# Gate and up units of the feed-forwards' groups 4 to 11 with seven products of quarters, their weight sums on VectorE

## The chip, the cores and the metric

The kernel runs on one core of one Trainium2 chip, in one launch. The metric is the device time of that core in microseconds (us), the median of several executions.

## The reference

Two transformer blocks follow each other on 512 tokens of 1024 features, with 16 further "meta" tokens ahead of them. Each block is a mixer (retention and stick-breaking heads in the first, two causal convolutions in the second) and then a feed-forward part. Everything is float32. The change touches only the two feed-forward parts:

```
def swiglu(hn, w_ffn_in, w_ffn_out):
    a, b = jnp.split(hn @ w_ffn_in, 2, axis=-1)
    return (jax.nn.silu(a) * b) @ w_ffn_out

def swiglu_2(xn, w_gate, w_up, w_down):
    a = jnp.einsum("btd,df->btf", xn, w_gate)
    u = jnp.einsum("btd,df->btf", xn, w_up)
    return jnp.einsum("btf,fd->btd", jax.nn.silu(a) * u, w_down)
```

The width `D_FF` is 2816. The input of each is `h` after an RMS norm with a gain; the kernel gives TensorE `h` times the gain and divides by the deviation (`std`) afterwards.

## The kernel before

**Products.** Float32 accuracy comes from splitting each operand into a high part in float32r and a low remainder: `mm3` (L600 to L602) makes three matmuls for every product, high by high, high by low and low by high. Weights come from memory as 140 "units" of 128x2048 numbers (1 MB each) in the order of their use, into two buffers `w_raw0` and `w_raw1` by turns. ScalarE rounds a unit to `w_hi` (`split_hi`, shown in the trace as L1159), VectorE makes `w_lo = w_raw - w_hi` (`split_lo`, L1721). There are two buffers of each too, so the buffer of a unit can be refilled for the unit after the next one as soon as TensorE has finished with it.

**The feed-forward.** Its 2816 hidden features are 11 groups of 256 (`FF_PAIRS`). A group has three units: gate (kind P, 8 tiles of 128 inputs by 256 outputs), up (P) and down (D, 2 tiles of 128 hidden features by 1024 outputs). TensorE's order is gate k, up k, down k-1, and the group after it. A P unit fills two "strips" (one PSUM bank of 128x512 each, 24 matmuls), a D unit eight (6 matmuls each). Every unit is 48 matmuls of 512 columns. PSUM banks go round in a ring of six: TensorE waits on `strip_free` before it takes a bank, and counts up `strip_done` when it has filled it.

**The rest of a group.** VectorE takes the gate strips out of PSUM while it divides by the deviation (`gate_in`, L2279). ScalarE makes the sigmoid (`silu_a`). VectorE multiplies (L2285), multiplies by the up strips (L2290), a tiny copy (L2293) tells ScalarE that `silu_a` is whole, ScalarE rounds it to `M_hi`, and VectorE makes `M_lo` (L2297). The eight strips of the down unit are added to `acc` one by one (L1982). Between these the in-order VectorE also makes the three `w_lo` of a group.

**Order.** It is written out by hand, engine by engine. `two` holds two groups and is the body of a hardware loop: five rounds in the first feed-forward, four and a copy in the second. Group 1 stands ahead of the loop (`up_first`), the down unit of group 11 behind it (`ffn_end`). SyncE issues the load of unit u when `w_lo` of unit u-2 is made, since that frees the `w_raw` buffer. GpSimd has no part in it but zeroing `acc`.

The trace calls two helpers' lines: L1159 is every ScalarE activation, L1738 every scalar_tensor_tensor of VectorE.

## Time and profile before

| | before |
|---|---|
| time, median of 3 runs | 1861.27 us (1861.24 to 1862.39) |
| the profiled execution's own span | 1859.4 us |
| TensorE busy (matmuls) | 1830.0 us, 98% |
| VectorE busy | 1132.7 us, 61% |
| ScalarE busy | 739.9 us, 40% |
| mean granted TensorE clock | 0.997 |

The span runs from the first to the last instruction of the profiled execution; the timed runs have about 1.9 us around it. Matmuls are pipelined, and one's duration in the trace is longer than the distance to the next one, so that TensorE's costs are read from start to start. The same holds, to a lesser degree, for VectorE: an instruction that waits for nothing starts before the end shown for the one ahead of it.

### The profile page before, as it was taken

To read this page: it belongs to the slowest core of one execution; us is meant where nothing else is said; L and a number is where in the kernel's file an instruction comes from. 1 tells how busy PE (TensorE), PEld (TensorE's weight loads), DVE (VectorE), ACT (ScalarE), POOL (GpSimd) and SP (SyncE) were. 2 spreads that over 40 slices of the span, in tenths; PEclk is the share of its full clock that TensorE was granted. 3 is DMA by queue.
4 is the path that set the end of the run, shared out by engine and by line. 5 is a ranking of instruction groups with operands and counts; after the bars stand their busy time and mean duration, and the time that the engine had idled before them with its cause. 6 is when DMAs were issued, how large, how long until landed. Compare 5 with 4: busy or idle time off the path is not lost.

```text
span 1859.4 us, 25253 instructions
## 1 busy us (share of the span) xinstructions
PE 1830.0 (98%) x10074; PEld 1586.4 (85%) x10074; DVE 1132.7 (61%) x1553; ACT 739.9 (40%) x927; POOL 33.5 (2%) x33
## 2 busy tenths in 40 slices
PE   9999999999999999999999999999999999999996
PEld 8898989889898888988888888888898888888885
DVE  7567566753736537357565454557898775554547
ACT  5666676532322333233442222224545742222222
POOL 2000000000000000000000000000000000000000
PEclk9999999999999999999999999999999999999998
DMA  4111111132122222222422222232476413222221
GB/s 184 38 64 59 45 45 46 59 112 103 46 90 79 90 96 72 70 69 91 161 69 95 105 93 90 90 113 88 114 183 170 126 69 113 90 93 104 96 91 46
DMA packets 25973, 170.07 MB, mean 91 GB/s; under 512 B 2736, under 2 KB 5040, under 8 KB 6320
## 3 DMA queue, kind: packets, MB, share of 16 engines
q1 hardware_dynamic: 24176, 156.51, 24.5%
q0 software_dynamic: 1728, 12.58, 3.3%
q8 instruction: 50, 0.82, 0.2%
q14 instruction: 19, 0.16, 0.0%
HBM read 154.40 MB, written 2.10 MB: 84 GB/s over the span
## 4 chain that ended last, share of the span: by engine, by line
PE 90%; DVE 5%; ACT 2%; issue 2%; DMA 0%; POOL 0%; DVEq 0%; SPq 0%; ACTq 0%
PE psum L600 28%; PE psum L601 28%; PE psum L602 28%; DVE normed L1738 1%; PE psum L751 1%; PE psum L802 1%; PE psum L797 1%; DVE h L1828 1%; ACT w_hi L1159 1%; ACT X_hi L1159 0%; PE psum L823 0%; DMA h<-in_xfm 0%; PE psum L1080 0%; ACT std L1159 0%; ACT sq L1159 0%
## 5 line engine op out<-in xcount | busy, mean ns | idle before, releaser
L600 PE MATMUL psum<-X_hi,w_hi 128*128 128x512 f32 (+2 forms) x1648 | 590.7, 358 | 3.1 <-issue 1.5
L602 PE MATMUL psum<-X_hi,w_lo 128*128 128x512 f32 (+2 forms) x1648 | 584.0, 354 | 0.0
L601 PE MATMUL psum<-X_lo,w_hi 128*128 128x512 f32 (+2 forms) x1648 | 584.0, 354 | 0.0
L1159 ACT ACTIVATE w_hi<-w_raw 128x2048 fp32r<-128x2048 f32 x133 | 253.8, 1909 | 357.9 <-PE psum L602 357.9
L600 PEld LDWEIGHTS psum<-X_hi,w_hi 128*128 128x128 f32 x1648 | 309.6, 188 | 51.5 <-issue 6.8
L1721 DVE TENSOR_TENSOR w_lo<-w_raw,w_hi 128x2048 fp32r<-128x2048 f32 x121 | 277.0, 2290 | 119.8 <-ACT w_hi L1159 119.8
L601 PEld LDWEIGHTS psum<-X_lo,w_hi 128*128 128x128 f32 x1648 | 310.0, 188 | 45.1 <-issue 2.4
L602 PEld LDWEIGHTS psum<-X_hi,w_lo 128*128 128x128 f32 x1648 | 309.6, 188 | 43.3
L1982 DVE TENSOR_TENSOR acc<-acc,psum 128x512 f32<-128x512 f32 x176 | 115.2, 685 | 46.9 <-PE psum L602 46.8
L600 PE MATMUL psum<-M_hi,w_hi 128*128 128x512 f32 (+2 forms) x376 | 141.4, 376 | 0.0
L601 PE MATMUL psum<-M_lo,w_hi 128*128 128x512 f32 (+2 forms) x376 | 141.0, 375 | 0.0
L602 PE MATMUL psum<-M_hi,w_lo 128*128 128x512 f32 (+2 forms) x376 | 141.0, 375 | 0.0
L600 PE MATMUL psum<-w_hi,X_hi 128*128 128x256 f32 x384 | 108.8, 283 | 0.0
L601 PE MATMUL psum<-w_lo,X_hi 128*128 128x256 f32 x384 | 108.6, 283 | 0.0
L602 PE MATMUL psum<-w_hi,X_lo 128*128 128x256 f32 x384 | 108.6, 283 | 0.0
L2279 DVE TENSOR_TENSOR gate_in<-psum,std 128x512 f32<-128x512 f32 x44 | 30.2, 691 | 112.0 <-PE psum L602 109.0
L1159 ACT ACTIVATE silu_a<-gate_in 128x512 f32<-128x512 f32 x44 | 27.6, 631 | 168.9 <-DVE gate_in L2279 168.9
L1738 DVE SCALAR_TENSOR_TENSOR z<-glu,vec,z 128x512 f32<-128x512 f32 x120 | 81.4, 742 | 0.5
L600 PEld LDWEIGHTS psum<-M_hi,w_hi 128*128 128x128 f32 x376 | 70.6, 188 | 13.0
L601 PEld LDWEIGHTS psum<-M_lo,w_hi 128*128 128x128 f32 x376 | 70.6, 188 | 12.9
L602 PEld LDWEIGHTS psum<-M_hi,w_lo 128*128 128x128 f32 x376 | 70.6, 188 | 12.7
L2290 DVE TENSOR_TENSOR silu_a<-silu_a,psum 128x512 f32<-128x512 f32 x44 | 29.9, 684 | 73.4 <-PE psum L602 73.4
(308 smaller groups left out, 2795.3 us busy)
## 6 DMA issues: line engine op xcount, KB each, us to landing
w_raw<-in_units SPq DMA_DIRECT2D x140, 1024.0 KB, 4.8
w_lo<-w_raw POOLq DMA_DIRECT2D x12, 1024.0 KB, 7.3
h<-in_xfm SPq DMA_DIRECT2D x4, 528.0 KB, 5.2
h<-in_xfm SPq DMA_DIRECT2D x1, 2112.0 KB, 9.1
decay<-in_dec SPq DMA_DIRECT2D x4, 512.0 KB, 4.7
out<-h SPq DMA_DIRECT2D x4, 264.0 KB, 2.2
out<-h SPq DMA_DIRECT2D x2, 496.0 KB, 2.9
rot<-in_consts SPq DMA_DIRECT2D x1, 528.0 KB, 13.0
```

The source lines that it names most:

```text
L600: nc.tensor.matmul(dst, w2[0], x2[0], start=first, stop=False, skip_group_check=True)
L601: nc.tensor.matmul(dst, w2[0], x2[1], start=False, stop=False, skip_group_check=True)
L602: m = nc.tensor.matmul(dst, w2[1], x2[0], start=False, stop=last, skip_group_check=True)
L751: m = nc.tensor.matmul(psum[0:rows, at.bank(s) + 1, 0:256], XM[:, k, meta], y[:, k, :], start=k == 0 and y is w[0], stop=k == DT - 1 and y ...
L797: m = nc.tensor.matmul(psum[:, 4 + b, 0:n], cmat[:, C_TRI, :], x[:, KEY_OFF[b]:KEY_OFF[b] + n], start=False, stop=False, skip_group_check= ...
L802: m = nc.tensor.matmul(psum[:, 4 + b, c0:c0 + KEY_LEN[b2]], cmat[:, C_ALL, :], x[:, KEY_OFF[b2]:KEY_OFF[b2] + KEY_LEN[b2]], start=False, s ...
L1159: return nc.scalar.activation(out_, in_, f, **kw)
L1721: v.tensor_tensor(lo, w_raw[at.ring(j)][:, :], as_f32(hi), ALU.subtract).then_inc(w_lo_ready, 1)
L1738: return v.scalar_tensor_tensor(out=out_, in0=in0, scalar=scalar, in1=in1, op0=op0, op1=op1)
L1982: v.tensor_tensor(dst[:, m, :], dst[:, m, :], strip_view(at.bank(s + n), SEQ), ALU.add)\
L2279: v.tensor_tensor(gate_in[:, c, :], strip_view(at.bank(s + c), SEQ), std[:, 0:SEQ], ALU.mult)\
L2290: v.tensor_tensor(silu_a[:, c, :], silu_a[:, c, :], strip_view(at.bank(s + 2 + c), SEQ), ALU.mult)\
```

## The change

In groups 4 to 11 of both feed-forwards (`k` from `FIRST7 = 3` to 10) each gate and up unit becomes kind S. Its 1024 inputs by 256 outputs by 512 tokens are cut in halves each way, and the result's four corners come from seven products of quarters instead of eight (Winograd's form of Strassen's method): a product is 4 tiles of 128 inputs, 128 outputs and 256 tokens, 12 matmuls of 256 columns. That is 84 matmuls of 256 columns in place of 48 of 512.

- Three of the products need sums of weight quarters (`wx_raw`, four tensor_tensor of 128x512 on VectorE, each waiting for the one ahead; the second overwrites a quarter of `w_raw`). They are split like weights: `wx_hi` by ScalarE (`sums_hi`), `wx_lo` by VectorE (`sums_lo`), 128x1536 each.
- Sums of the tokens' quarters (`T_hi`, `T_lo`, and one that replaces the lower late quarter of `X_hi`, `X_lo`) are made once in each feed-forward, during groups 2 and 3 (`two_whole`: `token_sums`, `token_lo`).
- The corners are put together on the way: ScalarE copies the first product out of PSUM (`takes`, "a"), VectorE adds the second to it ("u2"), the third to that ("u3") and the fourth ("c22"). TensorE then adds its last three products onto what stands in PSUM, and so waits in the midst of a unit, ahead of its fifth product for u2, ahead of the sixth for u3 and ahead of the seventh for c22. Two more VectorE steps finish the corners ("c21", "c12"), and the division by the deviation is now made from SBUF (`deviate`).
- The up result goes to SBUF (`up_in`) in the same way, and the product with it is one instruction of 128x1024.
- An S unit has three strips and the ring seven banks; TensorE takes a bank of an S unit only when all strips up to four behind are free.
- The table `rot` is loaded after the first norm instead of at the start, the `w_raw` load of unit 4 behind it. `h_sq` shares the place of `gate_in`, `first_hi` and `first_lo` share that of the new tiles.

TensorE in the first round of the loop, before (the middle of the gate unit) and now (around the fifth product); `wx_hi0` and `T_hi` are the sums:

```order
L620 ISA [waits w_lo_ready]
L600 MATMUL psum<-X_hi,w_hi0 128x512 [waits strip_free]
L601 MATMUL psum<-X_lo,w_hi0 128x512
L602 MATMUL psum<-X_hi,w_lo0 128x512
L600 MATMUL psum<-X_hi,w_hi0 128x512
```

```order
L649 MATMUL psum<-T_hi,w_hi0 128x256
L650 MATMUL psum<-T_lo,w_hi0 128x256
L651 MATMUL psum<-T_hi,w_lo0 128x256
L1127 ISA
L649 MATMUL psum<-X_hi,w_hi0 128x256 [waits c7_dve]
L650 MATMUL psum<-X_lo,w_hi0 128x256
L651 MATMUL psum<-X_hi,w_lo0 128x256
```

The unit no longer runs through: the fifth product waits for `c7_dve`, which VectorE counts up with u2.

VectorE from the end of a group's up unit to the next group's gate unit. Before, from the second up strip to the next `gate_in`, one row for each kind of step, without the register instructions between (the first `acc` row stands for three, the second for five):

```order
L2290 TENSOR_TENSOR silu_a<-silu_a,psum 128x512 [waits f_dve]
L2293 COPY silu_a<-silu_a 128x1 [waits strip_free]
L1982 TENSOR_TENSOR acc<-acc,psum 128x512 [waits strip_done]
L1721 TENSOR_TENSOR w_lo1<-w_raw1,w_hi1 128x2048 [waits w_hi_ready]
L2297 TENSOR_TENSOR M_lo<-silu_a,M_hi 128x1024 [waits f_act]
L1982 TENSOR_TENSOR acc<-acc,psum 128x512 [waits strip_done]
L1721 TENSOR_TENSOR w_lo0<-w_raw0,w_hi0 128x2048 [waits w_hi_ready]
L2279 TENSOR_TENSOR gate_in<-psum,std 128x512 [waits strip_done]
```

Now, the second half of the same stretch, from the last of the second four weight sums to u2 of the next gate unit, the last row (each `acc` row stands for two):

```order
L2456 TENSOR_TENSOR wx_raw<-w_raw0,wx_raw 128x512 [waits wx_second]
L2124 TENSOR_TENSOR acc<-acc,psum 128x512 [waits strip_done]
L2441 TENSOR_TENSOR M_lo<-silu_a,M_hi 128x1024 [waits f_act]
L2461 TENSOR_TENSOR wx_lo0<-wx_raw,wx_hi0 128x1536 [waits wx_hi_ready]
L2124 TENSOR_TENSOR acc<-acc,psum 128x512 [waits strip_done]
L1863 TENSOR_TENSOR w_lo0<-w_raw0,w_hi0 128x2048 [waits w_hi_ready]
L2529 TENSOR_TENSOR gate_in<-gate_in,psum 128x256 [waits c7_act]
```

From c12 of the up unit to u2 of the next gate unit there are now twenty instructions, where fourteen stood from the second L2290 to the next `gate_in`: c12, the product with the up result, `wx_lo` of the next gate unit, eight `acc` rows, two `w_lo`, four sums, `M_lo`, `wx_lo` of the next up unit, and u2, for which TensorE waits.

VectorE ahead of the first S unit, in the last part of `two_whole`:

```order
L2124 TENSOR_TENSOR acc<-acc,psum 128x512 [waits strip_done] x3
L1863 TENSOR_TENSOR w_lo0<-w_raw0,w_hi0 128x2048 [waits w_hi_ready]
L2450 TENSOR_TENSOR wx_raw<-w_raw1 128x512 [waits wx_lo_ready,w_loaded1]
L2452 TENSOR_TENSOR w_raw1<-w_raw1 128x512 [waits wx_first]
L2454 TENSOR_TENSOR wx_raw<-w_raw1 128x512 [waits wx_first]
L2456 TENSOR_TENSOR wx_raw<-w_raw1,wx_raw 128x512 [waits wx_second]
L2124 TENSOR_TENSOR acc<-acc,psum 128x512 [waits strip_done] x3
L2441 TENSOR_TENSOR M_lo<-silu_a,M_hi 128x1024 [waits f_act]
L2461 TENSOR_TENSOR wx_lo1<-wx_raw,wx_hi1 128x1536 [waits wx_hi_ready]
L2124 TENSOR_TENSOR acc<-acc,psum 128x512 [waits strip_done] x2
L1863 TENSOR_TENSOR w_lo1<-w_raw1,w_hi1 128x2048 [waits w_hi_ready]
```

`acc` takes the down unit's strips in threes; the first S unit of TensorE may take its bank only when the fourth of them is free, which is the first row of the second three, behind the four sums of the second unit.

The diff, cut:

```
+STRIPS = {"P": 2, "R": 4, "D": 8, "S": 3}
+FIRST7 = 3
+PAIRS7 = FF_PAIRS - FIRST7
+HT = SEQ // 2
...
+        if self.depth == 7:
+            return (j + 2) % 7
+        return (self.turn + j) % self.depth * max(1, 4 // self.depth)
...
-        loads(2, START["head0"][0] + 2)
+        loads(2, 4)
+        sync.wait_ge(x_lo_ready, DT)
+        constant(rot[:, :, :].rearrange("p a b -> p (a b)"), 0)
+        loads(4, START["head0"][0] + 2)
...
+            def seven(at, j, s, idx):
+                def taken(n):
+                    pe.wait_ge(strip_free, at.strip(s + n) - 4)
+                weights_ready(at, j)
...
+                early, late = slice(META, META + HT), slice(META + HT, FULL)
+                r1, r3 = (psum[:, at.bank(s), HT * i:HT * (i + 1)] for i in range(2))
+                r4, r2 = (psum[:, at.bank(s + i), 0:HT] for i in (1, 2))
+                def product(dst, ws, q, x, first, last, sig):
+                    for k in range(DT // 2):
+                        mm3(dst, [w[:, q, k * P:(k + 1) * P] for w in ws], x(k), first and k == 0,
+                            last and k == DT // 2 - 1, sig if k == DT // 2 - 1 else None)
...
+                taken(0)
+                product(r1, own, 0, own_x(0, early), True, False, None)
+                product(r3, added_to, 0, sum_x(1), False, True, c7_pe.step("P6"))
+                taken(1)
+                product(r4, added_to, 1, own_x(0, late), True, False, c7_pe.step("P7"))
+                taken(2)
+                product(r2, own, 2, sum_x(0), True, False, c7_pe.step("P5"))
+                pe.wait_ge(c7_dve.sem, c7_dve.at("u2", idx))
+                product(r1, own, 1, own_x(half, early), False, True, (strip_done, 1))
+                pe.wait_ge(c7_dve.sem, c7_dve.at("u3", idx))
+                product(r4, own, 3, sum_x(2), False, True, (strip_done, 1))
+                pe.wait_ge(c7_dve.sem, c7_dve.at("c22", idx))
+                product(r2, added_to, 2, own_x(half, late), False, True, (strip_done, 1))
...
+            def takes(at, s, idx, dst):
+                r1 = psum[:, at.bank(s), 0:HT]
+                act.wait_ge(c7_pe.sem, c7_pe.at("P6", idx))
+                a(dst[:, 0, 0:HT], r1, ACT.Copy).then_inc(*c7_act.step("a"))
+                strips(at, s)
+                act.wait_ge(c7_dve.sem, c7_dve.at("u2", idx))
+                a(dst[:, 0, 0:HT], r1, ACT.Copy).then_inc(strip_free, 1)
...
+                    takes(at, s + 3, index7(n, k, 1), up_in)
+                    strips(at, s + 5)
+                    if not last:
+                        sums_hi(at, 3 * m + 1, index7(n, k + 1, 0))
+                    split_hi(at, 3 * m + 1)
+                    act.wait_ge(f_dve.sem, f_dve.at("prod", base + k))
+                    hidden(base + k, (m + 1) % 2)
+                    if not last:
+                        sums_hi(at, 3 * m + 2, index7(n, k + 1, 1))
...
+            def sums_of(at, j, idx):
+                q = quarters(w_raw[at.ring(j)])
+                dve.wait_ge(w_loaded[at.ring(j)], 16 * (at.loads(j) + 1))
+                if not (type(idx) is int and idx == 0):
+                    dve.wait_ge(wx_lo_ready, idx)
+                v.tensor_tensor(wx_raw[:, 1, :], q[:, 0, :], q[:, 2, :], ALU.add).then_inc(*wx_first.step("s3"))
+                dve.wait_ge(wx_first.sem, wx_first.at("s3", idx))
+                v.tensor_tensor(q[:, 2, :], q[:, 2, :], q[:, 3, :], ALU.add).then_inc(*wx_first.step("s1"))
+                dve.wait_ge(wx_first.sem, wx_first.at("s1", idx))
+                v.tensor_tensor(wx_raw[:, 0, :], q[:, 0, :], q[:, 2, :], ALU.add).then_inc(*wx_second.step("s2"))
+                dve.wait_ge(wx_second.sem, wx_second.at("s2", idx))
+                v.tensor_tensor(wx_raw[:, 2, :], q[:, 1, :], wx_raw[:, 0, :], ALU.add).then_inc(*wx_second.step("s4"))
+            def sums_lo(at, j, idx):
+                dve.wait_ge(wx_hi_ready, idx + 1)
+                v.tensor_tensor(wx_lo[at.ring(j)][:, :, :], wx_raw[:, :, :], as_f32(wx_hi[at.ring(j)][:, :, :]), ALU.subtract)\
+                    .then_inc(wx_lo_ready, 1)
...
+                sums_of(at, 4, index7(n, FIRST7, 0))
+                dve.wait_ge(t_high.sem, t_high.at("t3_hi", n))
+                v.tensor_tensor(late_half(X_lo), T3_raw, as_f32(late_half(X_hi)), ALU.subtract).then_inc(*t_sums.step("t3_lo"))
+                sums_lo(at, 4, index7(n, FIRST7, 0))
+                add_down(at, 16, range(3))
+                split_lo(at, 4)
+                sums_of(at, 5, index7(n, FIRST7, 1))
+                add_down(at, 16, range(3, 6))
+                hidden_lo(i + 1, 0)
+                sums_lo(at, 5, index7(n, FIRST7, 1))
+                add_down(at, 16, range(6, DT))
+                split_lo(at, 5)
...
+            def chain(at, s, idx, dst):
+                dve.wait_ge(c7_act.sem, c7_act.at("a", idx))
+                v.tensor_tensor(dst[:, 0, HT:SEQ], dst[:, 0, 0:HT], psum[:, at.bank(s), HT:SEQ], ALU.add)\
+                    .then_inc(*c7_dve.step("u2"))
+                dve.wait_ge(c7_pe.sem, c7_pe.at("P7", idx))
+                dve.wait_ge(c7_dve.sem, c7_dve.at("u2", idx))
+                v.tensor_tensor(dst[:, 1, HT:SEQ], dst[:, 0, HT:SEQ], psum[:, at.bank(s + 1), 0:HT], ALU.add)\
+                    .then_inc(*c7_dve.step("u3"))
+            def corner22(at, s, idx, dst):
+                dve.wait_ge(c7_pe.sem, c7_pe.at("P5", idx))
+                dve.wait_ge(c7_dve.sem, c7_dve.at("u3", idx))
+                stt(dst[:, 1, HT:SEQ], psum[:, at.bank(s + 2), 0:HT], -1.0, dst[:, 1, HT:SEQ], ALU.mult, ALU.subtract)\
+                    .then_inc(*c7_dve.step("c22"))
+            def corner21(at, s, dst):
+                strips(at, s + 1)
+                dve.wait_ge(strip_free, at.strip(s) + 1)
+                stt(dst[:, 1, 0:HT], psum[:, at.bank(s + 1), 0:HT], -1.0, dst[:, 0, HT:SEQ], ALU.mult, ALU.subtract)\
+                    .then_inc(strip_free, 1)
+            def corner12(at, s, dst):
+                strips(at, s + 2)
+                dve.wait_ge(strip_free, at.strip(s + 1) + 1)
+                v.tensor_tensor(dst[:, 0, HT:SEQ], dst[:, 0, HT:SEQ], psum[:, at.bank(s + 2), 0:HT], ALU.add)\
+                    .then_inc(strip_free, 1)
+            def two(at, k0, final):
                 for m in range(2):
...
+                    k, s, i = k0 + m, 14 * m, base + k0 + m
+                    last = final and m == 1
+                    g, u = index7(n, k, 0), index7(n, k, 1)
+                    def deviate(c):
+                        dve.wait_ge(strip_free, at.strip(s + 2 - c) + 1)
+                        if c:
+                            dve.wait_ge(c7_dve.sem, c7_dve.at("c22", g))
+                        v.tensor_tensor(gate_in[:, c, :], gate_in[:, c, :], std[:, 0:SEQ], ALU.mult)\
+                            .then_inc(*g_dve.step(f"g{c}"))
+                    def gated(c):
+                        dve.wait_ge(f_act.sem, f_act.at(f"sig{1 - c}", i))
+                        v.tensor_tensor(silu_a[:, c, :], silu_a[:, c, :], gate_in[:, c, :], ALU.mult)\
+                            .then_inc(*f_dve.step(f"act{1 - c}"))
+                    chain(at, s, g, gate_in)
+                    corner22(at, s, g, gate_in)
+                    corner21(at, s, gate_in)
+                    deviate(1)
+                    corner12(at, s, gate_in)
+                    deviate(0)
+                    split_lo(at, 3 * m)
+                    chain(at, s + 3, u, up_in)
+                    gated(1)
+                    gated(0)
+                    corner22(at, s + 3, u, up_in)
+                    if not last:
+                        sums_of(at, 3 * m + 1, index7(n, k + 1, 0))
+                    corner21(at, s + 3, up_in)
+                    corner12(at, s + 3, up_in)
+                    dve.wait_ge(strip_free, at.strip(s + 5) + 1)
+                    dve.wait_ge(c7_dve.sem, c7_dve.at("c22", u))
+                    dve.wait_ge(f_dve.sem, f_dve.at("act1", i))
+                    v.tensor_tensor(silu_a[:, :, :], silu_a[:, :, :], up_in[:, :, :], ALU.mult)\
+                        .then_inc(*f_dve.step("prod"))
+                    if not last:
+                        sums_lo(at, 3 * m + 1, index7(n, k + 1, 0))
+                    add_down(at, s + 6, range(2))
                     split_lo(at, 3 * m + 1)
...
+                    add_down(at, s + 6, range(2, 4))
+                    if not last:
+                        sums_of(at, 3 * m + 2, index7(n, k + 1, 1))
+                    add_down(at, s + 6, range(4, 6))
+                    hidden_lo(i, (m + 1) % 2)
+                    if not last:
+                        sums_lo(at, 3 * m + 2, index7(n, k + 1, 1))
+                    add_down(at, s + 6, range(6, DT))
+                    if not (last and n):
                         split_lo(at, 3 * m + 2)
...
```

## Rows read from the trace of the kernel before

**Rows 1.** The page: busy time of each engine, share of the span, instructions.

```profile
PE 1830.0 (98%) x10074; PEld 1586.4 (85%) x10074; DVE 1132.7 (61%) x1553; ACT 739.9 (40%) x927; POOL 33.5 (2%) x33
```

**Rows 2.** The page: chain of work that ended last, by engine.

```profile
PE 90%; DVE 5%; ACT 2%; issue 2%; DMA 0%; POOL 0%; DVEq 0%; SPq 0%; ACTq 0%
```

**Rows 3.** Windows: busy of each engine, granted clock: one feed-forward, and the end.

```profile
core 0: us, PE busy (x) PEld busy (x) DVE busy (x) ACT busy (x) POOL busy (x), PEclk, DMA share, GB/s
970.00:1287.00 317.00, 316.29 (x1422) 262.88 (x1420) 170.74 (x197) 79.69 (x65) 0.00 (x0) 1.00 0.29 98
1848.00:1860.00 12.00, 0.00 (x0) 0.00 (x0) 8.49 (x22) 0.00 (x0) 0.00 (x0) 0.51 0.50 175
```

**Rows 4.** Timeline (start, duration): a down unit of 48 matmuls, the next unit, VectorE.

```profile
1005.11 0.39 PE L600 MATMUL psum<-M_hi,w_hi 128*128 128x512 f32 x1
...
1015.99 0.39 PE L600 MATMUL psum<-X_hi,w_hi 128*128 128x512 f32 x1
...
1016.19 0.69 DVE L1982 TENSOR_TENSOR acc<-acc,psum 128x512 f32<-128x512 f32 x1 [0.39 <-PE psum L602]
```

**Rows 5.** Timeline of TensorE: 256 columns, a start and the one 25 later.

```profile
35.09 0.28 PE L600 MATMUL psum<-w_hi,X_hi 128*128 128x256 f32 x1
...
38.09 0.28 PE L601 MATMUL psum<-w_lo,X_hi 128*128 128x256 f32 x1
```

**Rows 6.** Timeline of TensorE: 248 columns, a start and the one 8 later.

```profile
925.68 0.27 PE L600 MATMUL psum<-X_hi,M_hi 128*128 128x248 f32 x1
...
926.58 0.27 PE L602 MATMUL psum<-X_hi,first_lo 128*128 128x248 f32 x1
```

**Rows 7.** Timeline of VectorE in a round (start, duration, idle before and releaser).

```profile
1032.47 1.29 DVE L2285 TENSOR_TENSOR silu_a<-silu_a,gate_in 128x512 f32<-128x512 f32 x2
1033.68 0.68 DVE L2290 TENSOR_TENSOR silu_a<-silu_a,psum 128x512 f32<-128x512 f32 x1
1038.04 0.69 DVE L2290 TENSOR_TENSOR silu_a<-silu_a,psum 128x512 f32<-128x512 f32 x1 [3.68 <-PE psum L602]
1038.77 0.15 DVE L2293 COPY silu_a<-silu_a 128x1 f32<-128x1 f32 x1
...
1042.64 2.29 DVE L1721 TENSOR_TENSOR w_lo<-w_raw,w_hi 128x2048 fp32r<-128x2048 f32 x1
1044.84 1.22 DVE L2297 TENSOR_TENSOR M_lo<-silu_a,M_hi 128x1024 fp32r<-128x1024 f32 x1
1045.97 2.48 DVE L1982 TENSOR_TENSOR acc<-acc,psum 128x512 f32<-128x512 f32 x4
```

**Rows 8.** Lines by form of VectorE (count, busy, mean ns, idle before).

```profile
L2141 DVE TENSOR_TENSOR S_f<-psum,decay 128x256 f32<-128x256 f32 x4 | 1.7, 416 | 0.0
```

**Rows 9.** Lines by form of ScalarE.

```profile
L1159 ACT ACTIVATE w_hi<-w_raw 128x2048 fp32r<-128x2048 f32 x133 | 253.8, 1909 | 357.9 <-PE psum L602 357.9
L1159 ACT ACTIVATE silu_a<-gate_in 128x512 f32<-128x512 f32 x44 | 27.6, 631 | 168.9 <-DVE gate_in L2279 168.9
...
L1159 ACT ACTIVATE S_hi<-S_f 128x1280 fp32r<-128x1280 f32 x4 | 5.1, 1274 | 15.8 <-DVE S_f L2141 15.8
```

**Rows 10.** Timeline: VectorE releases TensorE amid narrow matmuls.

```profile
924.69 0.48 DVE L1738 SCALAR_TENSOR_TENSOR X_lo<-h,vec,X_hi 128x248 fp32r<-128x248 f32 x1 [0.23 <-ACT X_hi L1159]
...
925.23 0.38 PE L600 MATMUL psum<-X_hi,M_hi 128*128 128x248 f32 x1
...
925.45 0.28 PE L601 MATMUL psum<-X_lo,M_hi 128*128 128x248 f32 x1
```

**Rows 11.** Timeline of TensorE: an idle stretch amid a loop.

```profile
1331.96 0.28 PE L602 MATMUL psum<-X_hi,w_lo 128*128 128x264 f32 x1
1333.50 0.36 PE L600 MATMUL psum<-X_hi,w_hi 128*128 128x264 f32 x1 [1.27 <-issue]
```

**Rows 12.** Timeline of TensorE: the last matmuls of the kernel.

```profile
1843.91 1.05 PE L706 MATMUL psum<-sq,ones 128*128 128x264 f32 x4
```

**Rows 13.** The page: DMA issues (KB each, median us from issue to landing).

```profile
w_raw<-in_units SPq DMA_DIRECT2D x140, 1024.0 KB, 4.8
```

More of the change, by code:

```diff
@@ L1052, in ffn, with two @@
+            def two(at, k0):
+                whole = type(k0) is int and k0 == 1
+                for m in range(2):
+                    if whole:
+                        up(at, 3 * m, 12 * m)
+                    else:
+                        for c in range(2):
+                            seven(at, 3 * m + c, 14 * m + 3 * c, index7(n, k0 + m, c))
+                    down(at, 3 * m + 2, 12 * m + 4 if whole else 14 * m + 6, base + k0 - 1 + m, m)
             base = FF_PAIRS * n
             up_first(Place("ffn0" + tag, depth=6))
-            rounds = 5 if n == 0 else 4
@@ new lines, in token_sums @@
+            def token_sums(which):
+                for k in range(half):
+                    last = (lambda ins, name: ins.then_inc(*t_sums.step(name)) if k == half - 1 else ins)
+                    if which == "b12":
+                        last(v.tensor_scalar(t_raw[:, 0, k, :], x_part(k, 1), g_col(gain, k), None, ALU.mult), which)
+                    elif which == "t1":
+                        last(stt(t_raw[:, 1, k, :], x_part(k, 0), g_col(gain, k), t_raw[:, 0, k, :], ALU.mult, ALU.subtract), which)
+                    elif which == "t2":
+                        last(stt(t_raw[:, 2, k, :], x_part(half + k, 1), g_col(gain, half + k), t_raw[:, 1, k, :],
+                                 ALU.mult, ALU.add), which)
+                    elif which == "t4":
+                        last(stt(t_raw[:, 3, k, :], x_part(half + k, 0), g_col(gain, half + k), t_raw[:, 2, k, :],
+                                 ALU.mult, ALU.subtract), which)
+                    else:
+                        last(stt(T3_raw[:, k, :], x_part(half + k, 1), g_col(gain, half + k), t_raw[:, 0, k, :],
+                                 ALU.mult, ALU.subtract), which)
+                dve.wait_ge(t_sums.sem, t_sums.at(which, n))
```

176 lines of the change are left out of this document (133 added, 43 removed).

## Prediction, made before the changed kernel ran

> **What bounds the kernel now.** I read the page's engine rows first: TensorE is busy 98% of the span, VectorE 61%, ScalarE 40% [rows 1]. The chain of waits says the same, 90% of it is TensorE [rows 2]. Then I read the stage that the change touches: in 317 us of the first feed-forward TensorE is busy 316.29, VectorE 170.74, ScalarE 79.69, at a granted clock of 1.00, its upper level, 2.4 GHz [rows 3]. So a feed-forward costs its matmuls, from start to start. A unit of 48 matmuls takes 1015.99 - 1005.11 = 10.88 us [rows 4], a group of three 32.64. VectorE is busy 170.74/317 of it: 17.6 us of a group, and 15.0 free. The question is whether the work that the change gives it fits, and where in its order it stands.
>
> **TensorE's gain.** 84 matmuls of 256 columns take the place of 48 of 512. Matmuls of 256 columns stand 3.00/25 = 0.120 us apart [rows 5]; those of 248 columns, with X as here, 0.90/8 = 0.1125 [rows 6]; eight columns more at 2.4 GHz make that 0.116. I take 0.119: the first row has the very width. A product of 12 is 1.43 us, an S unit 10.0, a group 10.0 + 10.0 + 10.88 = 30.88, if TensorE never waits. The gain is 1.76 us in each of 16 groups, 28.2 us in all (16 at 0.120 gives 25.6, at 0.116 36.4).
>
> The Trainium skill ("TensorE: Matmul & The Clock Gate", "Back-to-back issue gap") gives the columns over 2.4 GHz and 2.5 ns more. That would be 0.109 us at 256 columns, an S unit of 9.2 us, and the sum below would come out at about 1858. The rows have 0.120, and 0.227 where the rule has 0.216, so I don't go by it.
>
> **What a VectorE step costs.** Two prices matter. Behind an instruction that it needn't wait for, the next one starts early: 512 columns cost 1.21/2 = 0.605, in the run of four `acc` 0.60; 1024 cost 1.13; 2048 cost 2.20 [rows 7]. So about 0.065 us and one column in 1.04 ns: 1536 columns 1.665, 256 columns 0.33. Where it waits for the one ahead, it costs the full duration and a gap: 1038.77 - 1038.04 = 0.73 for 512 [rows 7]; with 0.416 for 256 columns [rows 8], 0.46. By these prices all VectorE steps of a group add up to 29.2 us of TensorE's 30.9: eight sums 5.6, two `wx_lo` 3.3, ten corner steps about 4, three `w_lo` 6.6, eight `acc` 4.8, four gate steps 2.4, the product and `M_lo` 2.3. It fits by a hair in length; what decides is the order.
>
> **The loop that sets the pace.** TensorE's fifth product of a gate unit waits for u2, and u2 stands in VectorE's in-order queue behind all that it does after the up unit before. I walk from the end of that up unit (E). The release of VectorE takes 0.20 (`acc` starts at 1016.19, the next unit at 1015.99 [rows 4]). Then: c12 0.46, the 1024 product 1.13, `wx_lo` 1.665, two `acc` 1.20, `w_lo` 2.20, two `acc` 1.20, four chained sums 3 x 0.73 + 0.60 = 2.79, two `acc` 1.20, `M_lo` 1.13, `wx_lo` 1.665, two `acc` 1.20, `w_lo` 2.20, u2 itself 0.42. Sum 18.46; with the release 18.66. TensorE starts 0.06 behind VectorE's end and its second matmul comes 0.22 behind the first, not 0.11 [rows 10]: 18.83.
>
> TensorE's own way from E to that wait is the down unit, 10.88, and four products, 5.72: 16.60. So it stands still for 2.2 us in each group. The cycle closes: 18.83, then three products 4.29, then the up unit 10.0, is **33.1 us a group, against 32.64 before**. The gain of 1.76 is eaten by 2.2.
>
> Is anything later still? At the gate unit's end ScalarE needs 0.2 + 1.92 for the down unit's `w_hi` [rows 9], VectorE then `w_lo` 2.20 and u2 of the up unit 0.42: 4.8, TensorE asks at 5.72; no wait. From there VectorE has u3 0.46, two products 1.21, c22, four sums and c21, done 10.0 after the gate's end; c12 must wait for E + 0.2 anyway, so this part isn't the longer one, by 0.2 only. ScalarE's `wx_hi` (1.49, between 1.27 for 1280 columns and 1.91 for 2048 [rows 9]) ends 1.7 behind E, VectorE wants it at 1.9. ScalarE's sigmoids (0.63 each) and copies fit. Loads take 4.8 us [rows 13] and are wanted 11 us or more after the buffer is free. These edits cost nothing while VectorE's queue covers them; without that cover ScalarE's `wx_hi` would be late next.
>
> **The way in.** Group 3 keeps its old form, but VectorE has the token sums' low parts (three of 1.13), the late `X_lo`, and both units' sums in it. Counted from TensorE's start of group 3: gate strips until 11.7, `w_lo` 14.3 to 16.5, two products 17.7, three token parts 21.1, second up strip 22.7, four sums 25.6, `X_lo` 26.7, `wx_lo` (for which ScalarE sets 27.25) 28.9, three `acc` 30.7, `w_lo` 32.9, four sums 35.7, the fourth `acc` done 36.4. Only then may TensorE take a bank for the first S unit: at 36.5 instead of 32.64, 3.9 late. Its fifth product would start at 42.2, u2 is done at 44.1: 2.05 more.
>
> **The sum**, a feed-forward: 3.9 + (30.88 + 2.05) + 7 x 33.12 = 268.7, against 8 x 32.64 = 261.1: +7.6. Behind group 11 VectorE has no sums to make, `M_lo` is there 10.2 after the up unit, before the down unit's 10.88. Two feed-forwards: +15.2. The table `rot` and the second load are moved off the start; in a queue they stand behind what the start waits for, bounds -0.5 to +0.5, I take 0. The span goes from 1859.4 to 1874.6; the runs have 1.9 around it: **1876.5 us**, 0.8% slower.
>
> **Bounds.** The cycle is 18.83 and 120 matmuls: at 0.116 us apart it is 32.75, at 0.120 33.2 (-5 to +2 us in all 14 cycles). Register and wait instructions between VectorE's steps have no cost in the rows, but the 256-column steps have more of them; up to 0.1 for ten of them is +1.0 a group, +14 us. If short steps overlap more than the rows show (0.05 each of twenty) it is -1.0, -14.
>
> **Rivals.**
> *TensorE keeps its gain.* The walk decides by one number, E to TensorE's start: at 16.6 us or less no group waits. That wants VectorE's twenty steps 12% cheaper than [rows 7]. For it: the engine is at 61% in the whole kernel [rows 1]. Against it: columns at that rate fill 16.5 of the 18.46 us, and no row has a tensor_tensor faster than that. Time: 1861.3 + 2 x (3.9 - 8 x 1.76) = 1841. Chance 0.09.
> *Break-even.* The steps overlap more and the group falls to 32.2: 2 x (3.9 + 31.8 + 7 x 32.2 - 261.1) = 0, 1861. Chance 0.08.
> *No step starts early.* Each VectorE step then costs its full duration, 0.685 and 2.29 instead of 0.60 and 2.20 [rows 7], 15 of the twenty 0.09 more: +1.35 in each of 16 groups, 1898. [Rows 7] speak against it: four `acc` in 2.48. The Trainium skill ("VectorE: DVE Perf Modes", "The DRAIN you can't avoid") states it as a rule that the next op doesn't start until the pipe is empty; by that rule, 1898, and the trace disagrees. Chance 0.05.
> *The clock falls in the stalls.* After idle stretches of 1.3 us [rows 11] it stayed at 1.00; at the kernel's end it was down to 0.51 from 1848, some 3 us after the last matmul at 1845.0 [rows 12, 3]. A stall of 2.2 lies between. If it fell each time, three products at 1.2 GHz cost up to 4.3 more in 16 groups: over 1930. The one stall of 3.9 may well do it, but there the loss (up to 2 us) lies ahead of the wait for u2 and fills 2.05 of waiting. Chance 0.04.
>
> **How the numbers follow.** My forecast, VectorE sets the pace, has 0.74, from 1863 to 1892. A measurement of this kernel tells 0.2%, 3.7 us, from no change. Break-even is the same (0.08), the first rival faster (0.09), all else slower (0.83). Leaving out the first rival, the third and the fourth leaves 0.82, so the range runs from 1861 to 1892.
>
> **What would show it.** In the changed profile: TensorE idle, released by VectorE's `gate_in` line, once in each group of the loop, about 2.2 us long, and no such idle ahead of the up unit's fifth product; 33.1 us from gate unit to gate unit; 256-column matmuls 0.119 apart; VectorE over 90% busy in the loop; 3.9 us idle ahead of the first S unit, released by `acc`. No idle at u2 and 30.9 a group would prove me wrong, as would a VectorE step that differs from these rows by a tenth.

## The result, and the profile after

The changed kernel takes **1891.23 us** in the median (1889.55 to 1891.76, 4 runs) against 1861.53 (1861.24 to 1862.39, 4 runs) for the kernel before, a ratio of 1.0157 with a 95% interval of 1.0145 to 1.0169: 29.7 us slower. The forecast was 1876.5 with a range from 1861 to 1892. The direction was right and so, as the rows show, was the mechanism; the rise came out at twice the forecast one. The profiled execution has a span of 1889.2 us.

The page of the changed kernel, its first row (answers [rows 1]):

```profile
PE 1824.5 (97%) x11226; PEld 1636.9 (87%) x11226; DVE 1346.9 (71%) x1889; ACT 811.9 (43%) x1031; POOL 33.5 (2%) x33
```

The chain that ended last, by engine (answers [rows 2]):

```profile
PE 75%; DVE 16%; issue 6%; ACT 2%; DVEq 0%; POOL 0%; ACTq 0%; POOLq 0%
```

TensorE is still "busy" 97%, yet its share of the chain fell from 90% to 75% and VectorE's rose from 5% to 16%. The busy share hides it, since a matmul's shown duration is longer than its distance to the next, and covers part of each stall. The windows show it (answers [rows 3]; columns: stretch, length, busy of PE, PEld, DVE, ACT, POOL, granted clock, DMA share, GB/s). First the stretch of a whole feed-forward, then two single groups in it:

```profile
970.00:1287.00 317.00, 299.45 (x1912) 275.24 (x1911) 264.77 (x344) 109.53 (x108) 0.00 (x0) 0.97 0.26 93
1067.00:1101.00 34.00, 32.02 (x224) 29.92 (x224) 29.47 (x39) 11.84 (x12) 0.00 (x0) 1.00 0.26 93
1101.00:1134.00 33.00, 31.02 (x203) 28.92 (x203) 27.78 (x35) 11.79 (x12) 0.00 (x0) 0.95 0.26 95
```

VectorE is at 29.5 of 34 us; over six whole groups, 1061.51 to 1267.14, it is busy for 173.83 of 205.63 us, 85%. The granted clock reads 1.00 in one group and 0.95 in the next: that was not in the forecast, and it is most of the miss, 11.9 of 14.7 us. What TensorE waited for (line, releaser: us in total, times, longest):

```profile
PE psum L649 <- DVE gate_in L2529: 28.2, 16, 2.0
PE psum L649 <- DVE acc L2124: 7.1, 2, 3.6
```

Sixteen waits for u2 (L2529), one in each group of kind S, and two for `acc` (L2124), one on the way into each run of S units. Here they are on TensorE's timeline, with the first matmuls of the units in one group (start, duration, operation; in brackets the idle time before and its releaser):

```profile
1020.48 0.39 PE L649 MATMUL psum<-X_hi,w_hi 128*128 128x256 f32 x1 [3.56 <-DVE acc L2124]
...
1027.71 0.28 PE L651 MATMUL psum<-T_hi,w_lo 128*128 128x256 f32 x1
1028.21 0.39 PE L649 MATMUL psum<-X_hi,w_hi 128*128 128x256 f32 x1 [0.22 <-DVE gate_in L2529]
...
1061.51 0.38 PE L649 MATMUL psum<-X_hi,w_hi 128*128 128x256 f32 x1 [1.98 <-DVE gate_in L2529]
...
1063.31 0.41 PE L649 MATMUL psum<-X_hi,w_hi 128*128 128x256 f32 x1
1063.53 0.41 PE L650 MATMUL psum<-X_lo,w_hi 128*128 128x256 f32 x1
...
1096.30 0.39 PE L649 MATMUL psum<-X_hi,w_hi 128*128 128x256 f32 x1 [1.98 <-DVE gate_in L2529]
...
1100.71 0.28 PE L649 MATMUL psum<-X_hi,w_hi 128*128 128x256 f32 x1
...
1110.79 0.40 PE L649 MATMUL psum<-M_hi,w_hi 128*128 128x512 f32 x1
...
1121.70 0.28 PE L649 MATMUL psum<-X_hi,w_hi 128*128 128x256 f32 x1
...
1127.33 0.28 PE L651 MATMUL psum<-T_hi,w_lo 128*128 128x256 f32 x1
1129.60 0.39 PE L649 MATMUL psum<-X_hi,w_hi 128*128 128x256 f32 x1 [1.98 <-DVE gate_in L2529]
```

From fifth product to fifth product it is 1129.60 - 1096.30 = **33.30** us without a fall of the clock, and 1096.30 - 1061.51 = **34.79** with one. In the group of 34.79 the matmuls behind the stall stand 0.22 apart (1063.31, 1063.53), in the other 0.12: the clock is at its lower level, 1.2 GHz, for some 3.4 us (the granted clock reads 0.50 from 1061.86 to 1065.27), and 1.49 us is lost. In each feed-forward this happens in four of the seven stalls of 2.14 us, at 1061, 1130, 1198 and 1232 in the first. Why one such stall brings the clock down and the next does not, no run here shows. The same walk on VectorE, from c12 of the up unit to u2 of the next gate unit:

```profile
1110.99 0.42 DVE L2552 TENSOR_TENSOR up_in<-up_in,psum 128x256 f32<-128x256 f32 x1 [0.31 <-PE psum L651]
1111.55 1.23 DVE L2590 TENSOR_TENSOR silu_a<-silu_a,up_in 128x1024 f32<-128x1024 f32 x1
1112.69 1.75 DVE L2461 TENSOR_TENSOR wx_lo<-wx_raw,wx_hi 128x1536 fp32r<-128x1536 f32 x1
1114.36 1.28 DVE L2124 TENSOR_TENSOR acc<-acc,psum 128x512 f32<-128x512 f32 x2
1115.56 2.28 DVE L1863 TENSOR_TENSOR w_lo<-w_raw,w_hi 128x2048 fp32r<-128x2048 f32 x1
...
1126.93 2.28 DVE L1863 TENSOR_TENSOR w_lo<-w_raw,w_hi 128x2048 fp32r<-128x2048 f32 x1
1129.13 0.41 DVE L2529 TENSOR_TENSOR gate_in<-gate_in,psum 128x256 f32<-128x256 f32 x1
...
1134.36 0.42 DVE L1880 SCALAR_TENSOR_TENSOR gate_in<-psum,gate_in 128x256 f32<-128x256 f32 x1 [3.84 <-PE psum L651]
```

VectorE runs without idle from 1110.99 to 1129.54, with TensorE waiting at the end of it. Then, a moment later, it has 3.84 us with nothing to do. That free time right behind the critical step is what the experiments use.

Where the 29.8 us of span came from: the start is 0.7 later (the first matmul on X at 18.34 instead of 17.64), the first feed-forward is 14.7 longer, the stretch between 0.5 shorter, the second feed-forward 14.6 longer; 0.3 is spread over the rest.

### The profile page after: what moved, and what is told of

The parts are those of the page before. It is cut to its first block, busy times and chain, and to the rows that moved or that the text cites. A ratio compares the mean times of both kernels' runs of the same rounds, so it can differ in the third digit from the quotient of the medians.

```text
span 1889.2 us, 28279 instructions
## 1 busy us (share of the span) xinstructions
PE 1824.5 (97%) x11226; PEld 1636.9 (87%) x11226; DVE 1346.9 (71%) x1889; ACT 811.9 (43%) x1031; POOL 33.5 (2%) x33
## 4 chain that ended last, share of the span: by engine, by line
PE 75%; DVE 16%; issue 6%; ACT 2%; DVEq 0%; POOL 0%; ACTq 0%; POOLq 0%
PE psum L649 23%; PE psum L651 23%; PE psum L650 23%; DVE acc L2124 3%; DVE w_lo L1863 3%; DVE normed L1880 1%; DVE wx_lo L2461 1%; PE psum L800 1%; PE psum L851 1%; PE psum L846 1%; DVE h L1970 1%; DVE w_raw L2452 1%; DVE wx_raw L2454 1%; ACT w_hi L1250 1%; PE psum L771 1%
## 5 line engine op out<-in xcount | busy, mean ns | idle before, releaser
L649 PE MATMUL psum<-X_hi,w_hi 128*128 128x512 f32 (+2 forms) x1392 | 470.0, 338 | 38.1 <-DVE gate_in L2529 28.2
L651 PE MATMUL psum<-X_hi,w_lo 128*128 128x512 f32 (+2 forms) x1392 | 462.0, 332 | 0.0
L650 PE MATMUL psum<-X_lo,w_hi 128*128 128x512 f32 (+2 forms) x1392 | 461.6, 332 | 0.0
L649 PEld LDWEIGHTS psum<-X_hi,w_hi 128*128 128x128 f32 x1392 | 266.1, 191 | 71.0 <-DVE gate_in L2529 31.5
L650 PEld LDWEIGHTS psum<-X_lo,w_hi 128*128 128x128 f32 x1392 | 267.1, 192 | 25.7 <-issue 2.4
L651 PEld LDWEIGHTS psum<-X_hi,w_lo 128*128 128x128 f32 x1392 | 266.9, 192 | 23.5
L2124 DVE TENSOR_TENSOR acc<-acc,psum 128x512 f32<-128x512 f32 x176 | 113.0, 680 | 7.3 <-PE psum L651 7.1
L1250 ACT ACTIVATE wx_hi<-wx_raw 128x1536 fp32r<-128x1536 f32 x32 | 47.7, 1491 | 144.2 <-DVE wx_raw L2456 108.0
L651 PEld LDWEIGHTS psum<-M_hi,w_lo 128*128 128x128 f32 x376 | 70.6, 188 | 12.9
L649 PEld LDWEIGHTS psum<-M_hi,w_hi 128*128 128x128 f32 x376 | 70.6, 188 | 12.5
L649 PE MATMUL psum<-T_hi,w_hi 128*128 128x256 f32 x256 | 74.9, 293 | 0.0
L650 PE MATMUL psum<-T_lo,w_hi 128*128 128x256 f32 x256 | 74.5, 291 | 0.0
```

The lines of the kernel that those rows point to most:

```text
L649: nc.tensor.matmul(dst, w2[0], x2[0], start=first, stop=False, skip_group_check=True)
L650: nc.tensor.matmul(dst, w2[0], x2[1], start=False, stop=False, skip_group_check=True)
L651: m = nc.tensor.matmul(dst, w2[1], x2[0], start=False, stop=last, skip_group_check=True)
L1250: return nc.scalar.activation(out_, in_, f, **kw)
L2124: v.tensor_tensor(dst[:, m, :], dst[:, m, :], strip_view(at.bank(s + n), SEQ), ALU.add)\
```

## The experiments

Theory A throughout: VectorE's order sets the pace at u2, and the clock falls in part of the stalls. The rivals are named in each expectation: that VectorE is too full or too slow for any order to help, or that the losses have other causes. Ratios are to the kernel before on the same chip, whose median was 1861.61 us beside the two kernels with `w_lo` moved (alone, and with the bank freed earlier), the one with `M_lo` moved and the one with the extra step, and 1861.47 beside the other four.

### One `w_lo` moved behind c22

```
                 add_down(at, 16, range(6, DT))
-                split_lo(at, 5)
...
                     corner22(at, s, g, gate_in)
+                    split_lo(at, 3 * m - 1)
                     corner21(at, s, gate_in)
...
                     add_down(at, s + 6, range(6, DT))
-                    if not (last and n):
+                    if last and not n:
                         split_lo(at, 3 * m + 2)
```

The `w_lo` of the next group's up unit (2.20 us) goes from ahead of u2 into VectorE's idle time behind c22. The work is the same.

> VectorE's w_lo of the next up unit is made behind c22 of the next gate unit instead of ahead of u2; every step is kept. Theory A (VectorE's queue between the up unit's end and u2 sets the pace, and TensorE's stall there is what makes its clock fall): the queue is 2.2 us shorter, 16.35 us, so the stall of 2.14 us at the fifth product falls under 0.15, a group takes 31.2 us, and the clock falls no more than once in a feed-forward, in the idle time of 3.7 us ahead of the first S unit. Per feed-forward 3.7 + 1.5 - 8 x 1.48 = -6.6, time 1849. Theory B (TensorE is held by something else near there, a bank or a buffer, and w_lo only happens to end then): the stall stays at 2.1 or moves to the up unit, 1885 to 1895. Theory C (the clock falls because of the 256-column matmuls, not because of the stall): stall gone, but eight falls stay at 1.5 us each, 1861.

Measured: **1847.76 us** (1847.27 to 1849.3), ratio 0.9922 (0.9905 to 0.9938). The whole sign of the result turns on where one instruction stands. TensorE's one remaining wait in the S groups is the one for `acc` (its waits, first row); then a window on the way in and one in the loop, where VectorE is at 93%:

```profile
PE psum L649 <- DVE acc L2124: 7.1, 2, 3.6
```

```profile
1017.00:1034.00 17.00, 13.71 (x91) 13.71 (x92) 13.49 (x19) 4.57 (x5) 0.00 (x0) 0.80 0.24 76
1067.00:1101.00 34.00, 34.00 (x242) 32.12 (x241) 31.76 (x41) 12.54 (x14) 0.00 (x0) 1.00 0.27 97
```

That VectorE is too full for any order falls: it has more busy time in this window (31.76) than in the changed kernel (29.47), and nobody waits. The clock falls once in each feed-forward, in the wait of 3.56 us for `acc`, and stays down for 6.8 us there (1019.7 to 1026.5), twice as long as in the changed kernel. The first S unit takes 12.9 us in the first and 12.5 in the second feed-forward instead of 10.08: with no wait for u2 left to hide it, that fall costs 2.8 and 2.4 us.

### The same, and the bank freed earlier

```
-                add_down(at, 16, range(3))
+                add_down(at, 16, range(4))
                 split_lo(at, 4)
                 sums_of(at, 5, index7(n, FIRST7, 1))
-                add_down(at, 16, range(3, 6))
+                add_down(at, 16, range(4, 6))
```

In addition to the first move, VectorE takes four strips of the down unit ahead of `w_lo` and the four sums, so that the first S unit finds its bank free.

> As e1, and the fourth acc of the down unit ahead of the first S unit is added before the four sums of the second unit, not behind them. Theory A: the idle time ahead of the first S unit falls from 3.7 to about 1.0 us (then w_lo of that unit is last), the clock falls there no more, 2 x (1.0 - 8 x 1.48) = -21.7: 1840, faster than the kernel before. Theory B: as in e1, no gain over it. Theory C: 1852.

Measured: 1847.02 us (1845.32 to 1847.86), ratio 0.992 (0.9903 to 0.9937), where Theory A had wanted about 1840. A miss. Its timeline on TensorE and VectorE:

```profile
1017.61 0.38 PE L649 MATMUL psum<-X_hi,w_hi 128*128 128x256 f32 x1 [0.85 <-DVE w_lo L1863]
...
1025.84 0.39 PE L649 MATMUL psum<-X_hi,w_hi 128*128 128x256 f32 x1 [1.79 <-DVE gate_in L2528]
```

```profile
1015.19 2.28 DVE L1863 TENSOR_TENSOR w_lo<-w_raw,w_hi 128x2048 fp32r<-128x2048 f32 x1
1017.39 0.69 DVE L2450 TENSOR_TENSOR wx_raw<-w_raw 128x512 f32<-128x512 f32 x1
...
1021.37 1.22 DVE L2441 TENSOR_TENSOR M_lo<-silu_a,M_hi 128x1024 fp32r<-128x1024 f32 x1
...
1025.37 0.41 DVE L2528 TENSOR_TENSOR gate_in<-gate_in,psum 128x256 f32<-128x256 f32 x1
```

The wait at the bank shrank to 0.85, and one of 1.79 appeared at the fifth product of the same unit. VectorE runs without a pause from 1012.8 to u2 at 1025.37, so freeing the bank earlier doesn't shorten its queue. Behind this stall of 1.95 (start to start) the clock fell in the first feed-forward and not in the second. The expectation had treated the first wait as the only one on the way in. The profiled run, 1845.32, is the fastest of the four.

### The fourth `acc` alone

The second half of that diff, on the changed kernel.

> One part alone: in group 3 VectorE takes four strips of the down unit, not three, ahead of its w_lo and the four sums, so that the bank of the first S unit is free earlier. Theory A (VectorE is full through group 3, and what it saves at the bank it loses at u2 of the same unit): the stall ahead of the first S unit falls from 3.7 us to about 1, one of about 2 appears ahead of its fifth product, the end of that unit comes within 0.7 us of where it was: 1890 to 1891. Theory B (the two waits of the way in are costs of their own): 3 us less in each feed-forward, 1885.

Measured: 1894.79 us (1893.61 to 1896.26), ratio 1.0178 (1.0161 to 1.0195): **3.6 us slower** than the changed kernel, while Theory A had 1890 to 1891. Neither expectation held. The two ratios' intervals overlap a little; that the slowdown is real rests on the runs (none below 1893.61, none of the changed kernel above 1891.76) and on the trace:

```profile
1018.38 0.38 PE L649 MATMUL psum<-X_hi,w_hi 128*128 128x256 f32 x1 [0.85 <-DVE w_lo L1863]
...
1028.82 0.39 PE L649 MATMUL psum<-X_hi,w_hi 128*128 128x256 f32 x1 [4.00 <-DVE gate_in L2529]
...
1063.59 0.40 PE L649 MATMUL psum<-X_hi,w_hi 128*128 128x256 f32 x1 [1.98 <-DVE gate_in L2529]
```

Theory A's half about the overlap stands: the fifth product starts at 1028.82, against 1028.21 in the changed kernel, whose first matmul on X was 0.6 us earlier in its trace. But from there to the next fifth product it is 34.77 us, and in the changed kernel 33.30. The stall that brings the clock down now lies behind the first four products; the three that follow run at the lower level with nothing to hide it. In the changed kernel the fall came ahead of the first product, and its loss (those four products took 1027.83 - 1020.48 = 7.35 us instead of 5.75) filled time in which TensorE would have waited for u2 in any case. The first feed-forward is 1.5 us longer than in the changed kernel. The second is 2.3 longer: there the fall lasts 6.8 us, and from fifth product to fifth product it is 35.6 (1597.88 to 1633.48). Together that is 3.8 of the 4.4 us by which the two spans differ, and the later start is the other 0.6.

### `M_lo` moved instead of `w_lo`

```
                     corner22(at, s, g, gate_in)
+                    hidden_lo(i - 1, m)
...
-                    hidden_lo(i, (m + 1) % 2)
+                    if last:
+                        hidden_lo(i, (m + 1) % 2)
```

(and the same for the last group ahead of the loop): 1.13 us go from ahead of u2 to behind c22, half as much as `w_lo`.

> M_lo (1.13 us) is made behind c22 of the next gate unit in place of ahead of u2; w_lo stays where it was. Theory A: the stall at the fifth product falls by 1.13, from 2.14 to 1.0 us in each group, a group takes 32.2 us. If the clock falls only in longer stalls there are none in these groups: 2 x (3.7 + 1.5 + 7 x 1.0 - 11.8) = +0.8, 1862 to 1864. If it falls whatever the stall's length, eight falls of 1.5 stay: 1874.

Measured: 1868.5 us (1867.72 to 1870.08), ratio 1.0033 (1.0018 to 1.0049), some 5 above the expectation. VectorE in one group:

```profile
1087.45 1.28 DVE L2124 TENSOR_TENSOR acc<-acc,psum 128x512 f32<-128x512 f32 x2
1089.08 1.76 DVE L2461 TENSOR_TENSOR wx_lo<-wx_raw,wx_hi 128x1536 fp32r<-128x1536 f32 x1 [0.36 <-ACT wx_hi L1250]
...
1094.16 0.41 DVE L2528 TENSOR_TENSOR gate_in<-gate_in,psum 128x256 f32<-128x256 f32 x1
```

`M_lo` had stood where VectorE must wait for ScalarE's `wx_hi`; without it VectorE waits 0.36 there, and only 0.69 of 1.13 us arrives. The stall is 1.45 instead of 2.14, where the expectation had 1.0, the group 32.6 us, and the granted clock is 1.00 in every window from 1034 to 1268. So a stall of 1.45 us left the clock alone, where of seven of 2.14 four brought it down.

### One more VectorE step of 1024 columns

```
+                    dve.wait_ge(f_act.sem, f_act.at("M_hi", i))
+                    v.tensor_tensor(up_in[:, :, :], silu_a[:, :, :], as_f32(M_hi[:, (m + 1) % 2, :, :]), ALU.subtract)
                     hidden_lo(i, (m + 1) % 2)
```

> One more VectorE step of 128x1024 (the difference that makes M_lo, written once more to up_in, which is free then) ahead of u2. Theory A: the stall grows by 1.13 to 3.27 us, a group by 1.13: +16 us, 1907; if the clock falls at each longer stall instead of every second one, six more falls of 1.5 us: 1916. Theory B: the time stays within 3 us of the changed kernel's 1891.

Measured: 1915.93 us (1914.96 to 1916.91), ratio 1.0289 (1.0268 to 1.0309). The stalls, and two windows of about one group each:

```profile
PE psum L649 <- DVE gate_in L2529: 43.9, 16, 3.1
```

```profile
1134.00:1168.00 34.00, 32.80 (x216) 30.70 (x216) 28.19 (x38) 11.84 (x12) 0.00 (x0) 0.95 0.26 93
1168.00:1201.00 33.00, 30.01 (x196) 28.12 (x197) 27.38 (x36) 11.39 (x11) 0.00 (x0) 0.95 0.27 95
```

Each stall grew by the 1.13 us of the step, and now both of two neighbouring windows read 0.95: with a stall of 3.27 us the clock fell in every one of the seven groups of a feed-forward that have it, eight falls with the one on the way in. That is the 1916 that the expectation gave for this case.

### The stalls filled

```
+                if j in (0, 3):
+                    for n in range(16):
+                        nc.tensor.matmul(psum[:, 7, 0:HT], own[0][:, 2, 0:P], own_x(0, early)(0)[0], start=True,
+                                         stop=True, skip_group_check=True)
                 pe.wait_ge(c7_dve.sem, c7_dve.at("u2", idx))
```

The changed kernel with matmuls that nobody reads in its stalls: it takes the clock's part away and leaves VectorE's order as it is. First 16 of them, then 8.

> The changed kernel, with 16 more matmuls of 128x256 ahead of the wait for u2 in each gate unit of kind S, written to a PSUM bank that nobody reads (1.9 us of TensorE in a stall of 2.1). VectorE's order and TensorE's useful work stay the same. Theory A (VectorE sets the pace of 33.3 us a group, and the clock falls in every second stall of 2.1 us cost another 1.5 each): the fill hides in the stall, the remaining idle is 0.2 us, no half clock is left in the loops, all groups take 33.3 us; the kernel loses the 8 falls (12 us) and pays some 1.5 us in each first S unit, where the stall was 0.4: 1882. Theory B (the longer groups of 34.8 are longer because VectorE's steps took longer there, and the clock only shows it): the groups go on alternating, 1891 to 1894.

Measured: 1885.08 us (1884.98 to 1886.53), ratio 1.0126 (1.0109 to 1.0143). The profiled run (1886.53, the slowest of the four) lies 4.5 us above the expectation, and 3.7 of them lie outside the feed-forwards. A wait between units of the convolutions, amid work that the fills don't touch, is 2.8 us here and 1.2 in the changed kernel's trace, and a fall of the clock follows it (TensorE's waits, one row):

```profile
PE psum L649 <- issue: 3.4, 2, 2.8
```

> As the kernel with 16 more matmuls, but with 8 (0.96 us), so that 1.2 us of idle is left ahead of the fifth product in each group, less than the 1.45 at which no fall was seen. Theory A: no half clock in the loops, groups 33.3 us, and 0.6 us for each first S unit: 1880. Theory B: 1891 to 1894. A third outcome, falls in some groups only, would give 1882 to 1890.

Measured: **1881.97 us** (1880.94 to 1882.93), ratio 1.0111 (1.0094 to 1.0128). That is 2 above the expectation and at the very edge of its third outcome, falls in some groups only; the trace decides against that one. The waits and windows of the kernel with 8:

```profile
PE psum L649 <- DVE gate_in L2533: 14.1, 14, 1.0
```

```profile
1067.00:1101.00 34.00, 32.98 (x232) 30.88 (x231) 29.64 (x39) 12.44 (x13) 0.00 (x0) 1.00 0.27 93
1101.00:1134.00 33.00, 31.98 (x224) 29.88 (x224) 28.69 (x38) 11.58 (x13) 0.00 (x0) 1.00 0.26 95
```

In both kernels the clock is at 1.00 in every window of the loop, and the groups all take 33.30 us. TensorE does more work and the kernel is 9 us faster than the changed one, which settles that the longer groups of 34.79 were the clock's doing. With 8 fills the two feed-forwards are 5.45 and 4.64 us shorter than in the changed kernel: four falls of 1.49 are 5.96 in each, less 0.5 and 1.3 lost in the first S unit, where there was hardly a stall to hide the fills. (In the second feed-forward the fall on the way in also lasted longer than in the changed kernel: the four products took 8.14 us instead of 7.09, which is most of the 1.3.) With 16 fills 1.0 more is lost in each, and the two feed-forwards are 4.5 and 3.7 shorter. Filling half of the stall was enough.

### All three moves together

The `w_lo` move, the fourth `acc`, and `M_lo` behind c22 as well.

> Three moves together: w_lo of the next gate unit behind c22 of that gate unit, four strips ahead of the sums in group 3, and M_lo of the group before also behind c22 of the gate unit. Theory A: the loops have no stall, 30.9 us a group as with the first move alone; in the way in 1.13 us of VectorE's work goes out from ahead of u2 of the first S unit, so the 1.95 us that the first two moves left there fall to about 0.8, with no clock fall behind it: 2 x 1.1 to 2 x 2.3 less than their 1847.0, 1843 to 1845. Rival C: M_lo and w_lo together come too late for what follows c22 (u2 of the up unit, or the down unit that wants M_lo), a new wait in each group: 1850 to 1865.

Measured: **1842.44 us** (1841.85 to 1842.46), ratio 0.9898 (0.9881 to 0.9914), 19.0 us faster than the kernel before, the fastest of all and just below the 1843 to 1845 of the expectation.

```profile
PE 1806.2 (98%) x11226; PEld 1621.0 (88%) x11226; DVE 1345.6 (73%) x1889; ACT 811.4 (44%) x1031; POOL 33.4 (2%) x33
...
PE 88%; DVE 7%; ACT 3%; issue 2%; POOL 0%; DVEq 0%; ACTq 0%; POOLq 0%
```

```profile
1017.32 0.38 PE L649 MATMUL psum<-X_hi,w_hi 128*128 128x256 f32 x1 [0.85 <-DVE w_lo L1863]
...
1024.87 0.39 PE L649 MATMUL psum<-X_hi,w_hi 128*128 128x256 f32 x1 [1.11 <-DVE gate_in L2527]
```

```profile
1085.93 0.41 DVE L2527 TENSOR_TENSOR gate_in<-gate_in,psum 128x256 f32<-128x256 f32 x1
...
1116.99 0.41 DVE L2527 TENSOR_TENSOR gate_in<-gate_in,psum 128x256 f32<-128x256 f32 x1
```

The chain is TensorE's again (88%). A group takes 1116.99 - 1085.93 = 31.06 us, which is TensorE's own work, 2 x 10.08 + 10.91. On the way in the wait at u2 is 1.11 instead of 1.79, and no fall of the clock follows it. The sum: 8 x (32.64 - 31.06) = 12.6 gained in a feed-forward, and 3.0 lost on the way in (1.0 ahead of the bank, 0.5 in the four products, 1.3 at u2, 0.2 behind it). The trace has each feed-forward 9.7 shorter; twice that is 19.3, the median moved by 19.0.

## Why the prediction was right in kind and short in size

**VectorE's order as the limit: right, to 0.1 us.** From the down unit's start to TensorE's restart the forecast had 18.72 (18.46, 0.20 and 0.06); the rows have 1129.60 - 1110.79 = 18.81. The 0.09 are at one place: c12 to the product (1110.99 to 1111.55, 0.56 where 0.46 was taken), where several waits stand between the two; that the waits cost it wasn't tried apart. The bound for such waits, 0.1 at ten places, was ten times too wide. TensorE's own way was to be 16.60 and is 16.66 (1110.79 to 1127.33 and one spacing). The stall: 2.2 forecast, 2.14 measured, once in each group, and none ahead of the up unit's fifth product. That VectorE steps without a wait start early held too: 1024 columns 1.14, 1536 columns 1.67 (1112.69 to 1114.36), 2048 columns 2.20, all within 0.01 of the prices taken from [rows 7]. The Trainium skill ("VectorE: DVE Perf Modes", "The DRAIN you can't avoid") says that the next op does not start until the pipe is empty, and then that an op that is not held starts earlier. The forecast cited the rule without the exception, and called it contradicted. This trace shows the exception at work: `w_lo` is shown for 2.28 us, and u2 starts 2.20 behind it. One sign did not hold: VectorE "over 90% busy in the loop". It is at 85%. The forecast's own figures, 29.2 us of steps (its terms add up to 29.0) in a cycle of 33.1, give 88%, and the clock's falls lengthen the cycle further; against a group of 30.9 it would have been 94%.

**The spacing of 256-column matmuls: 0.119 taken, 0.120 measured.** An S unit is 1110.79 - 1100.71 = 10.08 us, where 10.0 was forecast. [Rows 5] had the very width and gave 0.120; I shaded it by the row of 248 columns, and the exact row was right. With the 0.09 above, the group is 33.30 instead of 33.12: some 2.5 us in the 14 cycles. The Trainium skill ("TensorE: Matmul & The Clock Gate", "Back-to-back issue gap") gives the columns over 2.4 GHz and 2.5 ns, 0.109 us at 256 columns, as the gap of isolated matmuls, and says that in a stream of weight loads and matmuls both set the spacing. By the isolated gap an S unit would take 9.2 us, an estimate; this trace, which is such a stream, has 10.08.

**The clock: the step that failed.** The forecast weighed "the clock falls in the stalls" as all or nothing, up to 4.3 us in each of 16 groups, over 1930, and gave it 0.04, because it had stayed at 1.00 after an idle stretch of 1.3 [rows 11]. A stall of 2.2 lay between the rows on either side, and the text said so; the partial case, some of the stalls and a smaller price, was not priced. It is the one that came: four of seven stalls in a feed-forward, at 1.49 us each, **11.9 us in all**, of the 14.7 by which the forecast was short. The price for one was three times too high as well: the lower clock lasted some 3.4 us, not for all of the three products behind the stall. The two kernels with filled stalls show that the longer groups are the clock's doing: without the falls all groups take 33.30. That 1891.23 still lies inside the range, by 0.8 us, is luck: the range's upper end was drawn for waits between VectorE's steps that came to 0.09 us a group, and the falls that filled it were priced outside.

**The way in: right, and right about the clock.** Forecast 3.9 late at the bank, measured 3.72 (3.56 by the bracket). At u2 of that unit 2.05 was forecast and 0.38 measured, but the four products between took 1.60 longer at the lower clock: together 1.98. The forecast had said that a fall there would be absorbed by the wait for u2. The kernel with the fourth `acc` alone shows the other side: put the stall behind those products, and the fall costs 1.5.

**The start: taken as 0, measured +0.7.** `w_raw`'s first half lands later (its cast starts at 12.54 instead of 11.84), and so does `h`: VectorE's sums for the norm end at 12.14 instead of 11.21. In the other eight traces with the changed order of loads the first matmul on X starts between 18.0 and 19.1, so it scatters by more than the difference, though all of them are later than the one trace of before. Which transfer delays it wasn't tried: `rot` now lies where `h` lies, so the old order of loads isn't open to this kernel. It stays open.

**The sum again.** 15.2 forecast; plus 11.9 for the falls, 2.5 for spacing and the one wait, 0.7 for the start, less 0.5 between the feed-forwards: 29.8, and the span grew by 29.8.

## What to carry to other kernels

When work moves from a full engine to a half-idle one, walk the in-order queue ahead of each step that the full engine waits for, with start-to-start prices; the busy share (71% here) tells nothing, and the cure is to move work from ahead of that step to the idle time right behind it, 2.20 us moved in each group being worth 43 us here, the falls of the clock that it ended included. Price a stall twice: its own length, and the slower matmuls behind it if the clock falls, in part of the stalls where the length lies between those that never and those that always bring it down. Before shortening the first of two waits on one path, ask when the second is due: it may take over the time, and put the clock's fall where nothing hides it.
